# Expert rows of token tile 0 worked on between the key choices of the query projections, with the gate matrices at row 216

## The reference, cut to what matters

```python
def peer_ffn(h, wq, subkeys, u, v):
    q = (h @ wq).reshape(B, S, 8, 2, 128)
    sub_scores = einsum('bshpk,hpnk->bshpn', q, subkeys)     # 2 x 128 scores a head
    top_v, top_i = lax.top_k(sub_scores, 16)                 # 16 keys of each half
    cand = top_v[..., 0, :, None] + top_v[..., 1, None, :]   # 16 x 16
    best_v, best_pos = lax.top_k(cand, 16)
    expert, gates = index_pair_of(best_pos), softmax(best_v)
    # for every token and each of its 8 x 16 experts:
    hid = gelu(u[expert] . h) * gates
    out = sum over experts of hid * v[expert]
```

## Time and profile before

| | us |
|---|---|
| median of three runs | 3074.04 |
| the profiled execution, own time | 3072.04 |
| its span, first to last instruction | 3070.1 |
| TensorE busy | 2822.9 (92%) |
| DVE busy | 1639.0 (53%) |
| GpSimd busy | 1341.7 (44%) |
| ACT busy | 919.7 (30%) |
| data moved | 586.50 MB |

### The profile page before, as it was taken

One profiled execution on the slowest core, in us unless ns is written; L12 is line 12 of the kernel. 1 busy time (PEld: TensorE's weight loads), 2 busy tenths in 40 slices (PEclk: granted clock), 3 DMA queues, 4 the chain that ended last, 5 costly groups with the idle time before them and its releaser, 6 DMA issues.

```text
span 3070.1 us, 32989 instructions
## 1 busy us (share of the span) xinstructions
PE 2822.9 (92%) x12386; PEld 2125.4 (69%) x12386; DVE 1639.0 (53%) x3114; ACT 919.7 (30%) x1701; POOL 1341.7 (44%) x979
## 2 busy tenths in 40 slices
PE   7989997899998989999897789999999999989964
PEld 6856886768788768888776678888888654434421
DVE  1032044843136243440305646999966999756676
ACT  3265244422434332222326332111112940000011
POOL 4422444734546224434242132344444954544465
PEclk9999998989999999999998899999999999999987
DMA  4300322003234116663331032899999379999998
GB/s 153 97 14 21 96 83 82 1 28 96 94 126 144 55 52 209 206 185 117 76 99 47 1 116 94 320 398 392 375 356 409 103 261 383 385 411 409 409 395 342
DMA packets 217519, 586.50 MB, mean 191 GB/s; under 512 B 23937, under 2 KB 48658, under 8 KB 216850
## 3 DMA queue, kind: packets, MB, share of 16 engines
q1 hardware_dynamic: 137312, 301.22, 28.8%
q0 software_dynamic: 74688, 271.61, 22.8%
q10 hardware_dynamic: 5362, 11.56, 1.2%
HBM read 576.98 MB, written 7.35 MB: 190 GB/s over the span
## 4 chain that ended last, share of the span: by engine, by line
PE 79%; DVE 8%; DMA 5%; ACT 3%; issue 2%; POOL 2%; SPq 0%; DVEq 0%; ACTq 0%; POOLq 0%
PE ps L1739 14%; PE ps L1235 14%; PE ps L1237 14%; PE ps L1236 14%; PE ps L1699 10%; DMA rows<-in_v,expert 3%; POOL rows L1154 2%; DMA rows<-in_u,expert 2%; PE ps L1313 1%; PE ps L1326 1%; PE ps L1727 1%; PE ps L1201 1%; PE ps L1253 1%; PE ps L1252 1%; PE ps L1251 1%
## 5 line engine op out<-in xcount | busy, mean ns | idle before, releaser
L1059 POOL TENSOR_TENSOR wlo<-wraw,whi 128x1024 fp32r<-128x1024 f32 x258 | 625.1, 2431 | 958.4 <-ACT whi L567 958.3
L567 ACT ACTIVATE whi<-wraw 128x1024 fp32r<-128x1024 f32 x258 | 270.8, 1058 | 818.6 <-PE ps L1237 702.0
L1739 PE MATMUL ps<-stream,hg 128*128 128x512 f32 x1024 | 442.3, 595 | 8.5 <-DMA stream<-in_v 8.5
L1235 PE MATMUL ps<-hhi,whi 128*128 128x512 f32 x1096 | 432.0, 394 | 18.2 <-DVE hlo L1851 5.9
L1699 PE MATMUL ps<-haff,stream 128*128 128x256 f32 x2048 | 444.1, 380 | 2.2 <-ACT stg L961 2.2
L1237 PE MATMUL ps<-hhi,wlo 128*128 128x512 f32 x1096 | 429.3, 392 | 0.0
L1236 PE MATMUL ps<-hlo,whi 128*128 128x512 f32 x1096 | 429.2, 392 | 0.0
L1699 PEld LDWEIGHTS ps<-haff,stream 128*128 128x128 f32 x2048 | 390.1, 191 | 55.7 <-ACT stg L961 2.4
L1739 PEld LDWEIGHTS ps<-stream,hg 128*128 128x128 f32 x1024 | 195.3, 191 | 255.5 <-issue 245.3
L1154 POOL DMA_INDIRECT rows<-in_u,expert x256 | 251.6, 983 | 262.7 <-DVE hid L2381 142.7
L2381 DVE CUSTOM_DVE_ANT_0 rows<-rows,h_s 128x1024 f32<-128x1024 f32 x256 | 313.1, 1226 | 96.9 <-DMA rows<-in_u,expert 91.6
(11 more groups left out here) (453 smaller groups left out, 4253.2 us busy)
## 6 DMA issues: line engine op xcount, KB each, us to landing
stream<-in_ut SPq DMA_DIRECT2D x128, 512.0 KB, 6.8
stream<-in_v SPq DMA_DIRECT2D x128, 512.0 KB, 6.8
wraw<-in_w_in SPq DMA_DIRECT2D x96, 512.0 KB, 3.7
wraw<-in_w_ada SPq DMA_DIRECT2D x48, 512.0 KB, 4.2
wraw<-in_w_gu SPq DMA_DIRECT2D x88, 256.0 KB, 3.8
wraw<-in_w_down SPq DMA_DIRECT2D x22, 512.0 KB, 3.6
wraw<-in_w_br_ssm SPq DMA_DIRECT2D x16, 512.0 KB, 3.6
wraw<-in_w_xkv SPq DMA_DIRECT2D x16, 512.0 KB, 4.0
```

What stands on the lines that cost most here:

```text
L567: act.activation(whi[:, n % WSLOTS, 0:kn, :], wraw[:, n % WSLOTS, 0:kn, :], ACT.Copy).then_inc(w_hi, 1)
L1059: pool.tensor_tensor(wlo[:, n % WSLOTS, 0:kn, :], wraw[:, n % WSLOTS, 0:kn, :], whi[:, n % WSLOTS, 0:kn, :].bitcast(F32), ALU.subtract).th ...
L1235: pe.matmul(dst, lh, rh, start=k == 0, stop=False)
L1739: ins = pe.matmul(ps[:, 2 * i + half, :], hg[:, n, P * i:P * i + P], stream[j][:, 4 * half:4 * half + 4, :], start=n == 0, stop=n == NKEYS ...
```

## The change

Seven edits, which belong together:

- `top_keys` of tile 0's heads 2 to 7 have rows between; only heads 0 and 1 have none. GpSimd gathers eight rows after the low parts up to the third query group, and then two after each low part of the last.
- The dense tiles' key choices go with blocks 3 to 10 and tile 1's with blocks 14 to 17 (before: 0 to 7 and 12 to 15); the score loads move accordingly.
- The order of four blocks changes: block 12 is u of head 7, 13 v of head 5, 14 v of head 6, 15 v of head 7 (tile 0), 16 u of tile 1's head 0.
- The gate matrices come after DVE's row (13, 7), so after 216 rows; the 16 rows in them are (13, 8) to (14, 7). The scaling of the dense gates goes from after block 10 to after block 12.
- Seven gelus instead of six stand among the u tiles, at tiles 4, 21, 47, 72, 88, 100, 116.
- TensorE takes 16 rows at the end instead of 32, half the rows of blocks 30 and 31.
- Four of the six gate operations (tiles 2 and 3) move from block 28 to block 29, the norm's steps back by two to four rows.

```diff
-    return order + [("v",) + blocks[-1][1:]]
+    order.append(("v",) + blocks[-1][1:])
+    for early, late in ((("v", 0, PEER_HEADS - 1), ("u", 1, 0)), (("u", 0, PEER_HEADS - 1), ("v", 0, PEER_HEADS - 3))):
+        first, last = order.index(late), order.index(early)
+        order[first], order[last] = order[last], order[first]
+    return order
...
-TOP_AFTER = {**{b: 4 + b for b in range(8)}, **{b: b for b in range(12, 16)}}
-MIX_AFTER = 11
+TOP_AFTER = {**{b: b + 1 for b in range(3, 11)}, **{b: b - 2 for b in range(14, 18)}}
+MIX_AFTER = (13, 7)
-GELU_AT = {21: 0, 40: 1, 66: 2, 91: 3, 107: 4, 118: 5}
-PE_HOLE = [(12, k) for k in range(TOPK)]
-PE_TAIL = [(b, k) for b in (26, 28, 30, 31) for k in range(1, TOPK, 2)]
+GELU_AT = {4: 0, 21: 1, 47: 2, 72: 3, 88: 4, 100: 5, 116: 6}
+PE_HOLE = [(13, k) for k in range(8, TOPK)] + [(14, k) for k in range(8)]
+PE_TAIL = [(b, k) for b in (30, 31) for k in range(1, TOPK, 2)]
...
# gpsimd_program
-            after("pq3")
+            after("pq1")
...
-            load_scores(0)
-            load_scores(1)
+            first = GROUPS[G["pq3"]][1]
+            rest_upto(first - 1)
+            for _ in range(RING):
+                gather_next()
+            for n in range(first, NCHUNK):
+                rest_upto(n)
+                for _ in range(2):
+                    gather_next()
             for b in range(len(BLOCKS)):
                 for k in range(TOPK):
-                    if k == RING and b == MIX_AFTER + 1:
+                    if k == 0 and b == MIX_AFTER[0] + 1:
                         pool.wait_ge(s("slots_ready"), 1)
...
+                    if k == RING and b == 2:
+                        load_scores(0)
+                        load_scores(1)
...
-                        if b - 1 - late in (12, 13):
-                            load_scores(TOP_AFTER[b - 1 - late] - 2)
+                        if b - 2 in (14, 15):
+                            load_scores(TOP_AFTER[b - 2] - 2)
...
# vector_program
+            def gate_matrices():
+
+                later_weights(PE_HOLE[-1][0])
+                v.wait_ge(s("slots_ready"), 1)
+                v.wait_ge(s("hg_ready"), NKEYS)
+                hots(0)
+                for m in range(ND // 4):
...
+            between_rows = {(12, 15): scale_gates, MIX_AFTER: gate_matrices,
+                            (28, 14): lambda: later_weights(30), (30, 4): lambda: later_weights(31),
+                            (28, 2): lambda: gate_sums(0), (28, 4): lambda: add_sums(0), (29, 7): lambda: gate_sums(2),
+                            (29, 9): lambda: add_sums(2), (29, 11): lambda: gate_sums(3), (29, 13): lambda: add_sums(3),
+                            (30, 10): lambda: root_begin((0, 1, 2)), (31, 2): lambda: root_end((0, 1, 2)),
+                            (31, 4): lambda: scaled_out((0,)), (31, 6): lambda: scaled_out((1,)), (31, 8): lambda: scaled_out((2,))}
...
-            for h in range(PEER_HEADS):
+            for h in range(2):
                 top_keys(0, h)
             v.wait_ge(s("h2_ready"), 2)
+            for h in range(2, PEER_HEADS):
+                top_keys(0, h, between=next_row)
```

More of the change, by code:

```diff
@@ L72 @@
 DVE_ROWS = [(b, k) for b in range(len(BLOCKS)) for k in range(TOPK) if (b, k) not in PE_ROWS]
+FIRST_DVE = {b: min(k for c, k in DVE_ROWS if c == b) for b in range(len(BLOCKS))}
 DIAGS, POOL_HOTS = 4, 4
@@ L1011, in scalar_program @@
                     act.activation(gates_d[:], gates_d[:], ACT.Exp).then_inc(s("gates_exp"), 1)
-                if n == NKEYS - 2 and PE_HOLE:
+                if n == NKEYS - 2:
                     row_diags(PE_HOLE[:DIAGS])
@@ L1032, in scalar_program @@
                 row_gelu(1, h)
-            row_diags(PE_TAIL[:8])
             row_gates(1, PEER_HEADS - 1)
             row_gelu(1, PEER_HEADS - 2)
-            row_diags(PE_TAIL[8:16])
+            row_diags(PE_TAIL[:DIAGS])
+            row_gelu(1, PEER_HEADS - 1, gates=False)
+            row_diags(PE_TAIL[DIAGS:8])
             tile_squares((0, 1, 2))
-            row_diags(PE_TAIL[16:16 + DIAGS])
-            row_gelu(1, PEER_HEADS - 1, gates=False)
-            row_diags(PE_TAIL[16 + DIAGS:24])
             tile_root((0, 1, 2))
-            row_diags(PE_TAIL[24:])
+            row_diags(PE_TAIL[8:])
             tile_squares((3,))
@@ L1173, in gather_next @@
                 gather(b, k)
-            late = 1 if PE_HOLE else 0
-            load_scores(0)
-            load_scores(1)
+            first = GROUPS[G["pq3"]][1]
[6 more added lines that the diff above has]
+                    gather_next()
             for b in range(len(BLOCKS)):
                 for k in range(TOPK):
-                    if k == RING and b == MIX_AFTER + 1:
+                    if k == 0 and b == MIX_AFTER[0] + 1:
                         pool.wait_ge(s("slots_ready"), 1)
@@ L1183, in gpsimd_program @@
                             first_hot(m)
-                            if PE_HOLE and m % 4 == 0 and m > 4:
+                            if m % 4 == 0 and m > 4:
                                 gather_next()
@@ L1728, in tensor_program @@
                 ins.then_inc(s("mix_mm"), 1)
-                if PE_HOLE and b % 4 == 1:
+                if b % 4 == 1:
                     row_half(b // 4, 0)
-                if PE_HOLE and b % 4 == 3:
+                if b % 4 == 3:
                     row_half(b // 4, 1).then_inc(s("pe_row_used"), 1)
@@ L2382, in next_row @@
                     return
-                if k == 0 and b in PE_BLOCKS:
-                    if b == PE_TAIL[0][0]:
+                if k == FIRST_DVE[b] and b in PE_BLOCKS:
+                    if b == PE_HOLE[0][0]:
                         head_weights(t, h).then_inc(s("wrow_ready"), 1)
@@ L2471, in later_weights @@
                 head_weights(*BLOCKS[b][1:]).then_inc(s("wrow_ready"), 1)
[L2473 to L2477, removed]
-            for h in range(PEER_HEADS):
+            def gate_matrices():
[4 more added lines that the diff above has]
+                for m in range(ND // 4):
+                    if m + 1 < ND // 4:
+                        hots(m + 1)
+                    mix(m)
+                    if m % 4 == 1 and 0 < m // 4 <= TOPK - DIAGS:
+                        hole_diagonal(DIAGS + m // 4 - 1)
+                v.wait_ge(s("pe_row_used"), TOPK)
+            between_rows = {(12, 15): scale_gates, MIX_AFTER: gate_matrices,
[5 more added lines that the diff above has]
+            for h in range(2):
                 top_keys(0, h)
             v.wait_ge(s("h2_ready"), 2)
+            for h in range(2, PEER_HEADS):
+                top_keys(0, h, between=next_row)
             for b, (kind, t, h) in enumerate(BLOCKS):
@@ L2491, in vector_program @@
                         between_rows[done]()
[L2492 to L2507, removed]
                 if (kind, t, h) == ("v", 0, PEER_HEADS - 1):
                     link(v.tensor_copy(h2_s[:, 0, :], own_sums(0)))
-                    if PE_HOLE:
-                        link(v.tensor_tensor(h2_s[:, 0, :], h2_s[:, 0, :], row_sums(1), ALU.add))
+                    link(v.tensor_tensor(h2_s[:, 0, :], h2_s[:, 0, :], row_sums(1), ALU.add))
             link(add_tile(1, own_sums(1)))
```

## The result

The changed kernel takes 3037.0 us (median of 4 runs, 3036.32 to 3039.09), the kernel before 3073.03 beside it on the same chip (3066.36 to 3074.09): a ratio of 0.989, 95% interval 0.9876 to 0.9903. The forecast was 3048, the range 3032 to 3064. The profiled execution of the changed kernel took 3036.32, its span is 3034.6; that of before was 3070.1, so 35.5 us are to be explained.

What follows compares the result with a forecast made beforehand. From 1930 us transfers are the full resource; the end is set by rows left at 2933 and each row's cost. 23.8 us (tail) + 2 (gate stage) = 25.8 off 3072.04 gives 3046.2, as a median 3048; range 3032 to 3064.

Steps and rivals of the forecast that it cites:

- Rival A: Tail: GpSimd sets the pace and DVE is never late; gain 36 + 2, 3036 us; chance 0.14.
- Step 1: Tile 0's key choices: first gather at 1877, first DVE row near 1884, u tiles still from 1930.2; 48 rows at 1995.
- Step 2: Up to row 216: DVE waits about 14 us at block 8, first gate matmul at 2378 to 2380; gain 2 us.
- The wait at block 8: Among the u tiles: DVE waits 14 us near 2188 for the gelu ACT does after u tile 72.
- Step 3: After the gate stage: DVE at row 442 instead of 418 when the v tiles end, near 2931; score loads cost 0.
- Step 4: Tail: GpSimd waits for DVE, not the reverse, from 2935 to 2993; 23.8 us gained.
- B: Before the gate stage: row 216 comes late, at 2.3 us a row instead of 1.99; 3058 us; chance 0.14.
- C: Early rows not done before 1930, row 216 still demanded and 49 us late; slower, 3097 (3099 as median); chance 0.06.
- D: The lead is lost elsewhere, half of C: within 0.3% of before; chance 0.06.

Runs made afterwards that it cites:

- the repeat: The kernel before and the changed kernel, both unchanged, built and run again: ratios to before 1.0004 and 0.9899 (3041.93 us).
- gelu_64: Changed kernel, but ACT does the gelu of head 3 after u tile 64 instead of 72; ratio to before 0.9889.
- tail_28: Changed kernel, but TensorE also takes half the rows of block 28, 24 rows at the end instead of 16; 3033.14 us, ratio to before 0.9876.
- no_early: Changed kernel without early rows: first gather behind the last low part, gelus of tile 0 moved, gate matrices still at row 216; 3070.68 us, ratio to before 0.9996.
- early_192: Changed kernel with early rows kept, but gate matrices, their hole, block order and later key choices back to row 192; 3077.98 us, ratio to before 1.0018.
- tail_26: Changed kernel, but TensorE takes half of blocks 26 and 28 too, 32 rows at the end as before; 3073.82 us, ratio to before 1.0002.

## Why the prediction was right, step by step

The forecast's mechanism was right: the early rows, a gate stage held by TensorE's u tiles and a tail with 24 rows fewer. Its size, 25.8 us against 26.4, is right for this pair of profiles, and that it comes so close is in part luck. The prediction took its tail from an execution of before in which it took 136.7 us; in the repeat it took 144.4, and the medians of the timed runs fell by 36.0 and, in the repeat, by 30.8 us. Against the median, the forecast of 3048 is 11 us too high. In the profiled execution 9.1 of these are the start of the u tiles, which moved with the execution; the other three runs have no trace, so for them this is argued, not shown. I treated the part ahead of 1877 us as fixed; one execution of each kernel gave no way to know its scatter of 10 us. Rival A, whose 3036 is nearest to the time, was not what happened, as the tail shows. What follows is in the time of the changed kernel; adding 9.1 gives the frame of the prediction.

**Step 1, the early rows.** The first gather is at 1867.74 (1876.9 in the old frame; predicted 1877) and the first row on DVE at 1873.99 (1883.1; 1884). GpSimd in order of time, cut to the first slow gather, the one ahead of it, and the four low parts:

```profile
1872.99 0.94 POOL L1157 DMA_INDIRECT rows<-in_u,expert  x1 [0.31 <-issue]
1874.24 1.80 POOL L1157 DMA_INDIRECT rows<-in_u,expert  x1 [0.30 <-issue]
...
1878.57 2.40 POOL L1062 TENSOR_TENSOR wlo<-wraw,whi 128x1024 fp32r<-128x1024 f32 x1
...
1885.03 2.41 POOL L1062 TENSOR_TENSOR wlo<-wraw,whi 128x1024 fp32r<-128x1024 f32 x1
...
1890.64 2.57 POOL L1062 TENSOR_TENSOR wlo<-wraw,whi 128x1024 fp32r<-128x1024 f32 x1
...
1895.93 2.36 POOL L1062 TENSOR_TENSOR wlo<-wraw,whi 128x1024 fp32r<-128x1024 f32 x1
```

The last low part, at 1895.93, corresponds to 1905.1 in the old frame (I said 1902), well ahead of TensorE's need, and the u tiles were not delayed by it. DVE in the same stretch:

```profile
1873.99 1.23 DVE L2392 CUSTOM_DVE_ANT_0 rows<-rows,h_s 128x1024 f32<-128x1024 f32 x1
...
1876.31 1.29 DVE L2392 CUSTOM_DVE_ANT_0 rows<-rows,h_s 128x1024 f32<-128x1024 f32 x1
...
1878.04 4.02 DVE L2392 CUSTOM_DVE_ANT_0 rows<-rows,h_s 128x1024 f32<-128x1024 f32 x1
```

The third row's operation spans a whole low part and takes 4.02 us, not 1.23. Head 2 took 27.8 us instead of 19.5, and the 48 rows were done at 2001.6 in the old frame: my sum had 1995. The Trainium skill's page "SBUF — State Buffer", section "Who interferes with whom", by which a DVE operation with two SBUF inputs and a GpSimd operation that reads SBUF exclude each other, gave 2002; the trace agrees: this row ends 1.1 us behind the low part, though its record starts 0.5 ahead of it. The low parts take 2.36 to 2.57 us as they do in the kernel before, so it was DVE that was held up and not they. As forecast it changed nothing behind it.

**Step 2, to row 216.** The wait at block 8 came where it was put (block 8 at 2188.4, predicted 2188), of 4.9 us instead of 14: it had swallowed the 7 us of step 1 and some 2 more. Row 176 at 2296.2 (2295.7), row 215 at 2370.1 (216 at 2372.5 to 2374), first gate matmul at 2378.5 (2378 to 2380). ACT's diagonals no longer stand in the way. The gain of 2.9 is the upper bound of 0 to 3: TensorE itself, at its last u tile, is now what sets it, as gelu_64 shows.

**Step 3.** DVE is at row 443 when the v tiles end (442 predicted), and the first score load behind the gate stage costs a wait of 3.9 us, the others none.

**Step 4, the tail.** DVE around rows 479 to 482:

```profile
2973.42 1.21 DVE L2392 CUSTOM_DVE_ANT_0 rows<-rows,h_s 128x1024 f32<-128x1024 f32 x1
...
2974.57 1.21 DVE L2392 CUSTOM_DVE_ANT_0 rows<-rows,h_s 128x1024 f32<-128x1024 f32 x1
2975.71 0.08 DVE L2392 DVE_READ_ACCUMULATOR2_ANT hid<- 128x1 f32 x1
2975.92 2.68 DVE L2406 SCALAR_TENSOR_TENSOR ps<-rows,wrow,ps 128x1024 f32<-128x1024 f32 x2
2981.87 1.29 DVE L2406 SCALAR_TENSOR_TENSOR ps<-rows,wrow,ps 128x1024 f32<-128x1024 f32 x1 [3.26 <-DMA rows<-in_v,expert]
```

DVE waits for nothing from 2921 until here, while GpSimd waits 4.6 us for DVE: DVE is the bound, as said. Two sizes were off and cancel. Rows that have landed follow each other at 1.145 us, not 1.28, so row 479 is done at 2975.8, 2984.9 in the old frame, where the sum had 2993, or 2991 with the 2 of step 2: 6 us sooner. But some ten gathers of the tail took 1.5 to 1.99 us where I had 0.94 (below), so GpSimd is by then 3.7 us late with row 487, at 2979.48, and it issues row 510 31.7 after it, at 3011.18 (29.4 predicted). That landed in 10.07 (10.4), and DVE's last row came at 3021.28; the prediction's 3032.9, less the 2 of step 2 and the 9.1 of the start, is 3021.8. The end of the tail was GpSimd's and the landings', as rival A has it, from row 480 on; up to there it was DVE's.

**The rivals.** A would have given 12 us more in the tail than the forecast; it did not come, and tail_28, which takes the bound off DVE in block 28, got 2 to 3 of it. B did not come: from row 176 (2287.07) to row 215 (2360.94) it was 73.9 us for 39 rows, 1.89 each. C is real as a mechanism (no_early) but came through the gate scaling and not through row 216, and was over-priced, as told. Its half, D, is what early_192 looks like: a lead that is waited away.

**What stays open.** Why the tail of before took 136.7 us once and 144.4 the other time. In the longer one GpSimd waits longer for TensorE's rows, and DVE for a late landing; which came first isn't settled. The tail of tail_26, which also begins with 425 gathers issued and has 32 rows on TensorE, took 145.9. If 144.4 is as usual as 136.7, the change is worth up to 8 us more than its profile pair says, and part of the timed 36 us would lie there. Nor is it known why the granted clock and the one wait of 6.1 us ahead of the u tiles differ between executions.

## What to carry to other kernels

A lead in one resource is worth what the next fixed point lets through: after work has been brought forward, move every gate behind it (here the gate matrices' row, the rows TensorE takes, the score loads), or the lead turns into a wait, as 57 us of waiting in early_192 and 50.6 in tail_26 did. Before a difference between two profiles is explained, count both from a mark that the change can't move; here 9 of 35 us fell away by that. And a slower rival is priced by following the work to its new place: a wait of the old place may fall away (14 us behind row 127 here), and an earlier demand of the same chain may come due first (the gate scaling behind row 207).

## What the runs showed of the hardware

GpSimd issues an indirect gather in 0.94 us, and now and then takes up to 1.99. The two lengths follow what DVE does at that moment. GpSimd in the tail of the kernel after:

```profile
2951.07 0.94 POOL L1157 DMA_INDIRECT rows<-in_u,expert  x1 [0.46 <-DVE ps L2406]
2952.61 1.67 POOL L1157 DMA_INDIRECT rows<-in_u,expert  x1 [0.60 <-issue]
2954.58 1.99 POOL L1157 DMA_INDIRECT rows<-in_u,expert  x1 [0.30 <-issue]
2956.87 1.99 POOL L1157 DMA_INDIRECT rows<-in_u,expert  x1 [0.31 <-issue]
2959.17 1.99 POOL L1157 DMA_INDIRECT rows<-in_u,expert  x1 [0.30 <-issue]
2961.46 0.94 POOL L1157 DMA_INDIRECT rows<-in_u,expert  x1 [0.30 <-issue]
```

and DVE beside it:

```profile
2951.06 1.28 DVE L2406 SCALAR_TENSOR_TENSOR ps<-rows,wrow,ps 128x1024 f32<-128x1024 f32 x1
2952.25 1.22 DVE L2392 CUSTOM_DVE_ANT_0 rows<-rows,h_s 128x1024 f32<-128x1024 f32 x1
...
2954.54 1.22 DVE L2392 CUSTOM_DVE_ANT_0 rows<-rows,h_s 128x1024 f32<-128x1024 f32 x1
...
2956.83 1.22 DVE L2392 CUSTOM_DVE_ANT_0 rows<-rows,h_s 128x1024 f32<-128x1024 f32 x1
...
2961.42 1.22 DVE L2457 TENSOR_TENSOR yout<-ps,gate2f 128x1024 f32<-128x1024 f32 x1
```

The gathers at 2954.58 and 2956.87 start 0.04 us into a u row, which reads two tiles from SBUF, and take 1.99; the gather at 2951.07 starts as close behind the start of a v row, and that at 2961.46 behind the start of a product, each with one input in PSUM, and take 0.94. Over the whole kernel before, 16 gathers take longer than 1.5 us: 14 start inside a u row and 2 inside an addition with both inputs in SBUF. The 47 that start inside a v row all take less than 1.05. Of the 45 that start inside a u row, those in its first 0.7 us take the longer the earlier they start (0.04 in, 1.99; 0.22 in, 1.82; 0.49 in, 1.54), so that they end about 2.03 us after the row's start, but for two that start at its first 0.04 us and take 0.94; the other 28 start in its last 0.2 us and take no more than 0.99. In the kernel after, 26 gathers take over 1.5 us (36 in its repeat), 10 of them in the tail in both executions, against 3 and 4 in the two of before. This is a coincidence in time seen in every trace, not an experiment: no run took the second input away. It costs up to a us each time a gather is GpSimd's next work and GpSimd is the bound, and by the sum of step 4 it is why the tail did not get all that DVE's quicker rows offered.
